# Conformer gates by the hyperbolic tangent, an earlier low part of the attention outputs, key copies from two queues

## The chip, the cores and the metric

The kernel runs on one core of one Trainium2 chip. The metric is the device time of one execution in microseconds; the kernel before took 2387.91 us in the median of 3 runs (2386.71 to 2388.96).

## The reference

One inference step of a two-layer streaming encoder, for 528 prompt frames (16 learned meta frames and 512) and 64 frames of a running stream, 592 columns in all. Per layer:

```python
xn = rmsnorm(x, p['norm1_g'])
proj = xn @ p['w_in']
q, k, v, sc_b, sc_c, sc_h, cf_a, cf_gate, gate_pre = jnp.split(proj, IN_SPLITS, axis=-1)
q = partial_rotary(q.reshape(n, l, N_Q_HEADS, HEAD_DIM), pos)
k = partial_rotary(k.reshape(n, l, N_KV_HEADS, HEAD_DIM), pos)
y_attn, new_k, new_v = attend(q, k, v, p['attn_sinks'])      # chunk-causal window, softmax with a sink per head
y_attn = y_attn @ p['w_attn_out']
...
glu = cf_a * jax.nn.sigmoid(cf_gate)
cf_conv, new_cf = causal_dwconv(glu, cf_hist, p['cf_conv_w'])    # 31 taps
y_cf = jax.nn.silu(layernorm(cf_conv, ...)) @ p['w_cf_out']
g_attn, g_sc, g_cf = jnp.split(jax.nn.sigmoid(gate_pre + p['b_gate']), 3, axis=-1)
x = x + (g_attn * y_attn + g_sc * y_sc + g_cf * y_cf) @ p['w_o']
...                                                              # a convolutional feed-forward block
```

D_MODEL is 1024, there are 16 query heads and 2 key/value heads of 64, and everything is float32.

## The kernel before, in words

Channels lie on the 128 partitions, frames along the free dimension. A weight matrix is cut into **panels** of 128 output channels by 1024 inputs, 174 per layer, which pass through in one fixed order. A panel is 8 **units** (one for each 128 inputs), and a unit is six matmuls: the float32 product is made of three passes, high weights by high input, high weights by low input, low weights by high input, each over two column pieces (L442). The high part of a panel's weights is written by ScalarE (`high`, L676), the low part by VectorE (`low`, L967); both have two buffers, so `high(w)` waits until TensorE has finished panel w-2, `low(w)` waits for `high(w)`, and TensorE waits for `low(w)` at the panel's first unit. SyncE issues the panels' loads.

Every engine's program is written out in order by hand, and each engine takes its instructions strictly in that order; waits are on semaphores. The change is in three places of a layer.

**The keys.** Panels 0 and 1 make keys and values, panels 2 to 9 the queries. The keys are rotated on VectorE (`k_rot`, L1046) and then copied twice into the buffer KD, one copy in each half of the partitions, by eight DMAs that SyncE issues one after another at panel 8 (L356, L357; for each of the 2 key heads and each half one large and one small). Before them on SyncE's queue stand the swaps for the first two queries and the load of panel 8, behind them the swaps for the next queries (L333, L334). ScalarE's `query(3)` (L733), which moves the result of a query panel out of PSUM into the place that the keys held, waits for all eight (`kd_in`), and TensorE's panel 7 waits for that PSUM tile. GpSimd copies the values (L400, L401) once VectorE has placed them (`vv_done`), and writes keys and values out after `kd_in`.

**The shade.** While TensorE runs panels 7 to 26 (160 units; the last queries and, as panels 10 to 25, eight pairs of a Conformer gate and a Conformer value), the attention is woven in. It has 20 items, one for each key head and chunk of frames; step s begins at unit 8 + 33 s // 5 (`STEP`), that is every six or seven units, and on TensorE it does `values(s - 3)`, `scores(s)`, `turn(s - 2)` (transposes). The other engines do their share at the same unit or one or two units (k) later:
- ScalarE at k = 1 `outputs_hi(s - 3)` and `copies(s - 2)`, at k = 2 `exps(s)` (one small and four large exponentials, L766 and L770);
- VectorE at k = 0 `divided(s - 1)` and `maxima(s)`, at k = 1 (and at k = 3 of odd steps, late in the shade) two convolution `taps` (L1157), and at k = 2 `outputs_lo(s - 3)` (L1119), the low part of an attention output.

TensorE's `scores(s)` waits for `exps(s - 1)`, since both use one PSUM region, and `values(i)` waits for `outputs_lo(i - 1)`. At each panel's start, ahead of the attention's share, ScalarE does `high` and then either a `query` or, at odd panels from 11 on, a Conformer gate: `gate` (L706), a Sigmoid from PSUM into scratch. VectorE does `low` and then a `rotation` of a query or, at even panels from 12 on, `glu` (L1141), the product of the gate and the value panel. Where a function that ScalarE needs is not in the table set that it holds, the compiled program has an ACT_TABLE_LOAD ahead of it; the profile gives it the line of the activation that needs it.

**Behind the shade**, panel 26 (N_OA) is the first of the branch gates, which are Sigmoids with a bias by the same `gate`.

Of the kernel before, what the change touches and what calls it, by code (L numbers as in the profile page):

```python
# [190 lines left out]
def encoder(nc, weights, xt, vecs, consts, kcache, vcache, cfhist, spill, y, kp, vp, scp, cfp, ffp, ks, vs):  # L191
# [18 lines left out]
    sums, rinv = sb("exp_sums", [128, 2, 4]), sb("inv_den", [128, 2, 4])  # L210
    warm = sb("warm", [128, 1])
    roots, inverse = sb("root_columns", [128, 2, 3]), sb("inverse_columns", [128, 2, 3])
# [68 lines left out]
    k_scaled, v_scaled, q_scaled, q1_tile = sem("k_scaled"), sem("v_scaled"), sem("q_scaled"), sem("q1_tile")  # L281
    k_cos, k_rot, kd_in = sem("k_cos"), sem("k_rot"), sem("kd_in")
    q_cos, q_sin, q_rot = sem("q_cos"), sem("q_sin"), sem("q_rot")
# [5 lines left out]
    o_done, oh_done, ol_done = sem("o_done"), sem("oh_done"), sem("ol_done")  # L289
    g_zero = sem("g_zero")  # L290
    tap_first, tap = sem("tap_first"), [sem(f"tap{g}") for g in range(4)]
# [16 lines left out]
    def tile_emptied(engine, key):  # L308
        s, before = USES[key]
        engine.wait_ge(out[s], before + 1)  # L310

    block = ctx.enter_context(nc.Block())
# [3 lines left out]
    def _(sp):  # L316
# [19 lines left out]
        for l in range(DEPTH):  # L336
            for n in range(PANELS):
# [13 lines left out]
                if n == 8:  # L351
                    sp.wait_ge(k_rot, l + 1)
                    for v in range(N_KV):
                        for h in (0, HEAD_DIM):
                            k = turning[HEAD_DIM * v:HEAD_DIM * v + HEAD_DIM, 0:TOK]
                            sp.dma_start(KD[h:h + HEAD_DIM, v, 0:TP], k[:, 0:TP]).then_inc(kd_in, 16)  # L356
                            sp.dma_start(KD[h:h + HEAD_DIM, v, TP + WINDOW:720], k[:, TP:TOK]).then_inc(kd_in, 16)  # L357
                if 8 <= n < 14:
# [15 lines left out]
    def _(pool):  # L374
        nc.gpsimd.memset(eps, EPS).then_inc(eps_set, 1)
        pool.dma_start(vs[:, 0:WINDOW - DEC_SEQ, :], vcache[:, DEC_SEQ:WINDOW, :]).then_inc(vs_out, 16)

# [8 lines left out]
        for l in range(DEPTH):  # L386
# [10 lines left out]
            pool.dma_start(VV[:, 7, 0, :], vcache[l, :, :]).then_inc(cache_in, 16)  # L397

            pool.wait_ge(vv_done, 2 * l + 2)
            pool.dma_start(VV[64:80, 0, 1, :], VV[0:16, 0, 1, :]).then_inc(v_twice, 16)  # L400
            pool.dma_start(VV[64:128, 1:8, 1, :], VV[0:64, 1:8, 1, :]).then_inc(v_twice, 16)  # L401
            pool.wait_ge(kd_in, (l + 1) * 128)
            pool.wait_ge(cache_in, (l + 1) * 32)
# [28 lines left out]
    def _(pe):  # L432
# [83 lines left out]
        def scores(l, i):  # L516
            v, c = divmod(i, CHUNKS)
            q0, k0, nk = chunk_span(c)
            g = l * ITEMS + i
            if i == 0:  # L520
                pe.wait_ge(q_rot, l * KT + 4)
                pe.wait_ge(vv_done, 2 * l + 2)
                pe.wait_ge(kd_in, (l + 1) * 128)
                pe.wait_ge(cache_in, (l + 1) * 32)
            if i == CHUNKS:
                pe.wait_ge(q_rot, l * KT + KT)
            if g:
                pe.wait_ge(p_done, g)
            for i2 in range(2):
                for e in range(2):  # L530
                    h = slice(64 * e, 64 * e + 64)
                    last = nc.tensor.matmul(scores_ps(nk)[:, e, i2, :], QI[h, 2 * v + i2, 2 * q0:2 * q0 + 128],  # L532
                                            KD[h, v, k0:k0 + nk], start=True, stop=True)
            last.then_inc(s_done, 1)
# [133 lines left out]
    def _(act):  # L668
# [33 lines left out]
        def gate(l, n, j, bias):  # L702
# [4 lines left out]
                .then_inc(out[USES[(l, n)][0]], 1)  # L707

        for m in range(KT):
            act.wait_ge(x_in[m], 16)  # L710
# [5 lines left out]
            square(m, m % 2, X[:, m, :], O_SQ, TOK)  # L716
        act.wait_ge(eps_set, 1)
        act.wait_ge(vec_in, 16)
        for l in range(DEPTH):
# [15 lines left out]
            def query(m):  # L735
                if m == 2:
                    act.wait_ge(vt_ps, 2 * l + 2)
                elif m == 3:
                    act.wait_ge(kd_in, (l + 1) * 128)
                elif m >= 4:  # L740
                    act.wait_ge(q_cos, l * KT + m - 3)
                    act.wait_ge(sw_in[place(m)], swaps(l, m - 4))
# [71 lines left out]
            for u in range(SHADE):  # L814
                n, k = N_SHADE + u // KT, u % KT
                if k == 0 and u:
# [3 lines left out]
                    elif (n - N_CF) % 2:  # L820
                        if n - N_CF >= 5:
                            tile_emptied(act, (l, n - 4))
                        gate(l, n - 1, (n - N_CF) // 2 % 2, 0.0)
                if n > N_CF and k == 5 and (n - N_CF) % 2 == 0:
# [132 lines left out]
    def _(dve):  # L957
# [46 lines left out]
        for l in range(DEPTH):  # L1004
# [118 lines left out]
            def attention_at(u):  # L1123
# [3 lines left out]
                if k == 0 and 0 <= s < ITEMS:  # L1127
                    maxima(s)
                if u > KT * (N_CF + 4 - N_SHADE) and (k == 1 or (k == 3 and s % 2)):
                    taps(1)  # L1130
                if k == 2 and 3 <= s:
                    outputs_lo(s - 3)

            def glu(m):
                tile_emptied(dve, (l, N_CF + 2 * m))
                dve.wait_ge(panel_done, W + N_CF + 2 * m + 2)
# [24 lines left out]
            for u in range(SHADE):  # L1161
                n, k = N_SHADE + u // KT, u % KT
                if k == 0 and u:
                    low(W + n + 1)
                    if n <= N_CF:
                        rotation(n - 2 - N_Q)
                    elif (n - N_CF) % 2 == 0:
                        glu((n - N_CF) // 2 - 1)
                if n == N_CF and k == 4:
                    rotation(KT - 1)  # L1170
                attention_at(u)

# [366 lines left out]
```

## Time and profile before

| | |
|---|---|
| median of 3 runs | 2387.91 us |
| the profiled execution | 2388.3 us, span 2387.0 us |
| TensorE matmuls busy | 2349.8 us (98%) |
| VectorE busy | 1598.5 us (67%) |
| ScalarE busy | 894.5 us (37%) |
| GpSimd busy | 43.6 us (2%) |
| mean granted TensorE clock | 0.998 of full speed |
| table loads | 52 of 1.283 us each, 38 of them at L706 and L766 |

The span runs from the first to the last instruction. An engine is busy while an instruction of its own executes; waiting for semaphores, and the issuing of DMAs, is not counted. Times in the trace are microseconds from the start of the span. The two layers are the same program; the second one's shade follows the first's by about 1191.7 us.

### The profile page before, as it was taken

The page shows a single profiled execution, that of the slowest core. Times are in us where ns is not written, and L with a number is a line of the kernel's source. Part 1 is how long each engine was busy: PE and PEld are TensorE (multiplying, and loading weights), DVE is VectorE, ACT ScalarE, POOL GpSimd, SP SyncE. Part 2 cuts the span into 40 slices and gives each one's busy share as a digit, 9 for nine tenths or more (in the row PEclk, how much of TensorE's full clock was granted, in tenths as well). Part 3 has the DMA queues.
Part 4 walks back from the last instruction along what each step waited for, and adds up shares of the span by engine and source line. Part 5 has one row for each costly group of instructions (what it writes and reads, how often), then busy time and mean ns, then how long its engine had stood idle before and what let it go on. Part 6 is the DMA issues. An engine that isn't in the chain of part 4 may idle for free.

```text
span 2387.0 us, 41935 instructions
## 1 busy us (share of the span) xinstructions
PE 2349.8 (98%) x17718; PEld 2313.9 (97%) x17718; DVE 1598.5 (67%) x2386; ACT 894.5 (37%) x1725; POOL 43.6 (2%) x74
## 2 busy tenths in 40 slices
PE   8999999999999999999999999999999999999998
PEld 8988999999999999999998889999999999999997
DVE  8677798885535664645776778999764356556366
ACT  5566222223523432423435662222244234334243
POOL 2000000000000000000010000000000000000000
PEclk9999999999999999999999999999999999999999
DMA  6211222222232222222242112222223322222222
GB/s 209 82 54 54 82 82 80 80 81 80 93 103 85 80 80 81 85 83 81 90 138 80 54 54 84 81 89 80 80 81 104 97 88 80 87 82 80 84 84 96
DMA packets 60028, 205.97 MB, mean 86 GB/s; under 512 B 8702, under 2 KB 10974, under 8 KB 59582
## 3 DMA queue, kind: packets, MB, share of 16 engines
q1 hardware_dynamic: 56448, 191.23, 24.8%
q0 software_dynamic: 3392, 12.05, 1.7%
q8 instruction: 140, 2.29, 0.4%
q14 instruction: 48, 0.39, 0.1%
HBM read 191.77 MB, written 8.50 MB: 84 GB/s over the span
## 4 chain that ended last, share of the span: by engine, by line
PE 91%; DVE 4%; ACT 2%; issue 1%; SPq 1%; DMA 1%; DVEq 0%; ACTq 0%
PE ps L442 87%; PE ps L532 1%; DVE w_lo L967 1%; PE ps L547 1%; PE ps L564 1%; ACT w_hi L676 1%; DVE xn_hi_lo L984 0%; DVE x_q_merged L1011 0%; PE ps L568 0%; ACT scratch L770 0%; DMA scratch<-cf_acc 0%; DVE scratch L979 0%; PE ps L470 0%; PE ps L550 0%; DVE cf_acc L1157 0%
## 5 line engine op out<-in xcount | busy, mean ns | idle before, releaser
L442 PE MATMUL ps<-xn_hi_lo,w_hi 128*128 128x288 f32 (+3 forms) x7552 | 1334.7, 299 | 12.9 <-DVE w_lo L967 9.6
L442 PEld LDWEIGHTS ps<-xn_hi_lo,w_hi 128*128 128x128 f32 x7552 | 1115.6, 188 | 15.8 <-issue 10.6
L442 PE MATMUL ps<-xn_hi_lo,w_lo 128*128 128x304 f32 (+2 forms) x3776 | 816.6, 298 | 0.0
L676 ACT ACTIVATE w_hi<-raw 128x1024 fp32r<-128x1024 f32 x348 | 369.3, 1061 | 1081.6 <-PE ps L442 1080.5
L967 DVE TENSOR_TENSOR w_lo<-raw,w_hi 128x1024 fp32r<-128x1024 f32 x348 | 426.0, 1224 | 519.6 <-ACT w_hi L676 519.4
L442 PEld LDWEIGHTS ps<-xn_hi_lo,w_lo 128*128 128x128 f32 x3776 | 605.7, 188 | 0.0
L442 PE MATMUL ps<-branch_hi_lo,w_hi 128*128 128x304 f32 (+2 forms) x2896 | 509.6, 298 | 4.3 <-DVE branch_hi_lo L1315 1.7
L442 PEld LDWEIGHTS ps<-branch_hi_lo,w_hi 128*128 128x128 f32 x2896 | 426.8, 188 | 7.1 <-issue 2.2
L1157 DVE SCALAR_TENSOR_TENSOR cf_acc<-glu,vec,cf_acc 128x622 f32<-128x622 f32 x480 | 383.6, 860 | 0.0
L442 PE MATMUL ps<-branch_hi_lo,w_lo 128*128 128x288 f32 (+2 forms) x1448 | 311.9, 297 | 0.0
L442 PEld LDWEIGHTS ps<-branch_hi_lo,w_lo 128*128 128x128 f32 x1448 | 232.2, 188 | 0.0
L1319 DVE SCALAR_TENSOR_TENSOR scratch<-scratch,vec 128x594 f32<-128x594 f32 x176 | 147.1, 836 | 18.6 <-ACT scratch L906 11.9
L1295 DVE TENSOR_TENSOR x_q_merged<-x_q_merged,ps 128x592 f32<-128x592 f32 (+2 forms) x62 | 47.3, 763 | 162.2 <-PE ps L442 162.0
L906 ACT ACTIVATE scratch<-scratch,vec 128x594 f32<-128x594 f32 x88 | 70.0, 796 | 153.4 <-DVE scratch L1325 153.4
L442 PE MATMUL ps<-merged_hi_lo,w_hi 128*128 128x288 f32 (+2 forms) x512 | 90.0, 298 | 0.3 <-DVE w_lo L967 0.2
L442 PEld LDWEIGHTS ps<-merged_hi_lo,w_hi 128*128 128x128 f32 x512 | 75.5, 188 | 0.7 <-issue 0.7
L1325 DVE TENSOR_TENSOR scratch<-scratch,ps 128x64 f32<-128x64 f32 (+2 forms) x176 | 72.2, 452 | 0.0
L770 ACT ACTIVATE scratch<-ps,neg_max 128x192 f32<-128x192 f32 (+3 forms) x160 | 60.0, 390 | 0.0
L442 PE MATMUL ps<-merged_hi_lo,w_lo 128*128 128x288 f32 (+2 forms) x256 | 55.3, 297 | 0.0
L975 DVE TENSOR_TENSOR scratch<-scratch 128x592 f32<-128x592 f32 (+1 forms) x54 | 42.1, 779 | 1.0
L984 DVE SCALAR_TENSOR_TENSOR xn_hi_lo<-x_q_merged,vec,xn_hi_lo 128x592 fp32r<-128x592 f32 x48 | 38.8, 827 | 4.6 <-ACT xn_hi_lo L713 4.6
L792 ACT ACTIVATE branch_hi_lo<-ps 128x128 fp32r<-128x128 f32 x80 | 17.8, 275 | 63.6 <-PE ps L550 50.3
(138 smaller groups left out, 1322.7 us busy)
## 6 DMA issues: line engine op xcount, KB each, us to landing
raw<-in_weights SPq DMA_DIRECT2D x348, 512.0 KB, 3.4
spill<-x_q_merged POOLq DMA_DIRECT2D x2, 2368.0 KB, 9.7
x_q_merged<-spill POOLq DMA_DIRECT2D x16, 296.0 KB, 3.1
x_q_merged<-in_xt SPq DMA_DIRECT2D x8, 296.0 KB, 7.0
cf_acc<-cf_acc SPq DMA_DIRECT2D x72, 18.5 KB
out_y<-x_q_merged SPq DMA_DIRECT2D x4, 304.0 KB, 2.4
out_y<-x_q_merged SPq DMA_DIRECT2D x4, 288.0 KB, 2.3
scratch<-cf_acc SPq DMA_DIRECT2D x8, 132.0 KB, 3.7
```

The costliest lines, as they stand in the source:

```text
L442: last = nc.tensor.matmul(to[:, t0:t1], a[:, w % 2, wk], both[:, part, k, t0:t1], start=(k == 0 and j == 0), stop=(k == nk - 1 and j == 2))
L532: last = nc.tensor.matmul(scores_ps(nk)[:, e, i2, :], QI[h, 2 * v + i2, 2 * q0:2 * q0 + 128], KD[h, v, k0:k0 + nk], start=True, stop=True)
L676: nc.scalar.activation(wh[:, w % 2, :], raw[:, w % 2, :], ACT.Copy).then_inc(hi_done, 1)
L770: last = nc.scalar.activation(scr[:, O_P + 768 * b + 192 * x:O_P + 768 * b + 192 * x + nk], scores_ps(nk)[:, x // 2, x % 2, :], ACT.Exp, b ...
L906: nc.scalar.activation(dst, src[:, 0:S_OUT], ACT.Identity, bias=0.0, scale=col(l, "ffw", m * 3)) \
L967: V.tensor_tensor(wl[:, w % 2, :], raw[:, w % 2, :], f(wh[:, w % 2, :]), ALU.subtract).then_inc(lo_done, 1)
L975: V.tensor_tensor(view(at, n), view(at, n), slot(sq, CF_OUT, s)[:, 0:n], ALU.add).then_inc(sq_sum, 1)
L984: V.scalar_tensor_tensor(xl[:, m, :], X[:, m, :], col(l, g, m), f(xh[:, m, :]), ALU.mult, ALU.subtract) \
L1157: V.scalar_tensor_tensor(acc[:, t, :], G[:, t, k + 1:k + 1 + CF_OUT], col(l, "cfw", t * CF_K + k + 1), acc[:, t, :], ALU.mult, ALU.add).th ...
L1295: V.tensor_tensor(X[:, m, t:], X[:, m, t:], ps((l, n0 + m))[:, t:], ALU.add) \
L1319: V.scalar_tensor_tensor(dst, src[:, k:k + S_OUT], col(l, "ffw", m * 3 + k), dst, ALU.mult, ALU.add) \
L1325: last = V.tensor_tensor(dst[:, o:o + w_], view(O_RF + t0_, w_), ps(key)[:, t0_:t0_ + w_], ALU.mult)
```

## The change

Three things, in both layers.

The Conformer gates become `sigmoid(x) = 0.5 tanh(x / 2) + 0.5`: a Tanh with scale 0.5 out of PSUM, a wait for its own end, and an Identity with scale 0.5 and a bias column of 0.5 in place. `glu` waits for the Identity by a semaphore of its own; the PSUM tile is still given free by the first of the two.

On VectorE, `outputs_lo(s - 3)` moves from k = 2 to k = 0, behind `maxima(s)` and ahead of the taps. At unit 8, the shade's first step, `maxima(0)` moves ahead of the rotation of a query.

Of the eight key copies, SyncE issues the four of key head 0 and GpSimd the four of key head 1, which there stand ahead of the copies of the values. The semaphore is split; the scores of key head 1 wait for theirs at item 10, ScalarE's `query(3)` and GpSimd's output of the keys wait for both.

```diff
-    k_cos, k_rot, kd_in = sem("k_cos"), sem("k_rot"), sem("kd_in")
+    k_cos, k_rot, kd_in = sem("k_cos"), sem("k_rot"), [sem("kd_in0"), sem("kd_in1")]
...
+    def keys_twice(engine, v):
+
+        k = turning[HEAD_DIM * v:HEAD_DIM * v + HEAD_DIM, 0:TOK]
+        for h in (0, HEAD_DIM):
+            engine.dma_start(KD[h:h + HEAD_DIM, v, 0:TP], k[:, 0:TP]).then_inc(kd_in[v], 16)
+            engine.dma_start(KD[h:h + HEAD_DIM, v, TP + WINDOW:720], k[:, TP:TOK]).then_inc(kd_in[v], 16)
...
                 if n == 8:
                     sp.wait_ge(k_rot, l + 1)
-                    for v in range(N_KV):
-                        for h in (0, HEAD_DIM):
-                            k = turning[HEAD_DIM * v:HEAD_DIM * v + HEAD_DIM, 0:TOK]
-                            sp.dma_start(KD[h:h + HEAD_DIM, v, 0:TP], k[:, 0:TP]).then_inc(kd_in, 16)
-                            sp.dma_start(KD[h:h + HEAD_DIM, v, TP + WINDOW:720], k[:, TP:TOK]).then_inc(kd_in, 16)
+                    keys_twice(sp, 0)
...
         nc.gpsimd.memset(eps, EPS).then_inc(eps_set, 1)
+        nc.gpsimd.memset(half[:, :], 0.5).then_inc(half_set, 1)
...
+            pool.wait_ge(k_rot, l + 1)
+            keys_twice(pool, 1)
             pool.wait_ge(vv_done, 2 * l + 2)
...
+        def tanh_gate(l, n, j):
+
+            act.wait_ge(panel_done, l * PANELS + n + 1)
+            to = slot(O_SG, TOK, j)
+            nc.scalar.activation(to, ps((l, n)), ACT.Tanh, scale=0.5).then_inc(out[USES[(l, n)][0]], 1)
+            tile_emptied(act, (l, n))
+            nc.scalar.activation(to, to, ACT.Identity, bias=half[:, :], scale=0.5).then_inc(sigmoid_done, 1)
...
-                        gate(l, n - 1, (n - N_CF) // 2 % 2, 0.0)
+                        tanh_gate(l, n - 1, (n - N_CF) // 2 % 2)
...
                     maxima(s)
+                if k == 0 and 3 <= s:
+                    outputs_lo(s - 3)
                 if u > KT * (N_CF + 4 - N_SHADE) and (k == 1 or (k == 3 and s % 2)):
                     taps(1)
-                if k == 2 and 3 <= s:
-                    outputs_lo(s - 3)
...
             def glu(m):
-                tile_emptied(dve, (l, N_CF + 2 * m))
+                dve.wait_ge(sigmoid_done, l * KT + m + 1)
...
                 if k == 0 and u:
                     low(W + n + 1)
+                if u == KT:
+                    attention_at(u)
+                if k == 0 and u:
                     if n <= N_CF:
                         rotation(n - 2 - N_Q)
...
-                attention_at(u)
+                if u != KT:
+                    attention_at(u)
```

## Rows read from the trace of the kernel before

**Rows 1.** The page, part 1: busy time, share, instructions.

```profile
PE 2349.8 (98%) x17718; PEld 2313.9 (97%) x17718; DVE 1598.5 (67%) x2386; ACT 894.5 (37%) x1725; POOL 43.6 (2%) x74
```

**Rows 2.** First layer's shade by stretch: length, PE, PEld, DVE, ACT, POOL busy, PEclk.

```profile
73.00:242.00 169.00, 163.46 (x1394) 149.38 (x1393) 120.38 (x274) 105.38 (x309) 0.00 (x0) 1.00 0.17 56
```

**Rows 3.** PE's waits, whole span: line, releaser, us in total, times, longest.

```profile
PE ps L532 <- ACT scratch L770: 6.9, 6, 1.4
PE ps L564 <- DVE branch_hi_lo L1119: 4.0, 6, 1.2
PE ps L442 <- ACT cf_acc L733: 3.2, 4, 1.4
```

**Rows 4.** PE's timeline: start, us, line, operation, [idle before, releaser].

```profile
61.25 0.80 PE L442 MATMUL ps<-xn_hi_lo,w_hi 128*128 128x304 f32 x4 [0.78 <-ACT cf_acc L733]
...
68.00 0.62 PE L532 MATMUL ps<-scratch,x_q_merged 64*128 64x16 f32 x8
...
74.58 0.68 PE L532 MATMUL ps<-scratch,x_q_merged 64*128 64x80 f32 x8 [0.86 <-ACT scratch L770]
...
121.49 0.92 PE L532 MATMUL ps<-scratch,x_q_merged 64*128 64x192 f32 x8 [1.40 <-ACT scratch L770]
...
168.99 0.65 PE L564 MATMUL ps<-scratch 16*64 16x128 f32 x8 [1.17 <-DVE branch_hi_lo L1119]
...
1252.92 0.81 PE L442 MATMUL ps<-xn_hi_lo,w_hi 128*128 128x304 f32 x4 [1.43 <-ACT cf_acc L733]
```

**Rows 5.** ACT's timeline ahead of PE's wait of 1.40 us.

```profile
115.25 1.28 ACT L706 ACT_TABLE_LOAD   x1
116.55 0.66 ACT L706 ACTIVATE scratch<-ps 128x592 f32<-128x592 f32 x1
...
118.33 1.28 ACT L766 ACT_TABLE_LOAD   x1
```

**Rows 6.** Groups by line, whole span: count, busy us, mean ns, idle before.

```profile
L706 ACT ACT_TABLE_LOAD x22 | 28.2, 1283 | 0.4
L766 ACT ACT_TABLE_LOAD x16 | 20.5, 1283 | 0.3
L693 ACT ACTIVATE xn_hi_lo<-x_q_merged,vec 128x592 fp32r<-128x592 f32 x24 | 18.6, 775 | 0.0
```

**Rows 7.** DVE's timeline ahead of PE's wait of 1.17 us.

```profile
164.91 1.23 DVE L967 TENSOR_TENSOR w_lo<-raw,w_hi 128x1024 fp32r<-128x1024 f32 x1 [1.35 <-ACT w_hi L676]
...
168.36 0.48 DVE L1119 TENSOR_TENSOR branch_hi_lo<-ps,branch_hi_lo 128x128 fp32r<-128x128 f32 x2
```

**Rows 8.** ACT's timeline at the same place: the second of the two `copies`.

```profile
165.40 0.25 ACT L783 ACTIVATE scratch<-ps 16x128 f32<-16x128 f32 x1
```

**Rows 9.** DVE's timeline ahead of PE's wait of 0.86 us.

```profile
69.26 1.23 DVE L967 TENSOR_TENSOR w_lo<-raw,w_hi 128x1024 fp32r<-128x1024 f32 x1 [1.81 <-ACT w_hi L676]
...
72.66 0.22 DVE L1081 TENSOR_REDUCE score_max<-ps 128x4 f32<-128x64 f32 x1
```

**Rows 10.** SP's timeline: the fourth of the eight key copies.

```profile
54.22 0.60 SPq L357 DMA_DIRECT2D scratch<-cf_acc  x1
```

**Rows 11.** The chain that ended last: from the eighth key copy to query(3).

```profile
56.80 3.70 DMA scratch<-cf_acc
...
60.53 0.67 ACT cf_acc L733
```

**Rows 12.** POOL's timeline: its copies of the values.

```profile
54.62 0.53 POOL L400 DMA_DIRECT2D scratch<-scratch  x1 [22.09 <-DVE scratch L1065]
55.14 0.78 POOL L401 DMA_DIRECT2D scratch<-scratch  x1
```

**Rows 13.** DMA issues by line: queue, count, KB each, median us to landing.

```profile
scratch<-scratch POOLq DMA_DIRECT2D x2, 224.0 KB, 4.5
```

**Rows 14.** DVE's timeline: the end of the keys' rotation, and of query 3's.

```profile
51.23 0.78 DVE L1046 TENSOR_TENSOR cf_acc<-cf_acc 128x592 f32<-128x592 f32 x1
...
65.80 0.77 DVE L1056 TENSOR_TENSOR cf_acc<-cf_acc,cos_sin 128x592 f32<-128x592 f32 x1 [0.66 <-DMA cf_acc<-cf_acc]
```

More of the change, by code:

```diff
@@ L210, in encoder @@
     sums, rinv = sb("exp_sums", [128, 2, 4]), sb("inv_den", [128, 2, 4])
-    warm = sb("warm", [128, 1])
+    warm, half = sb("warm", [128, 1]), sb("half", [128, 1])
     roots, inverse = sb("root_columns", [128, 2, 3]), sb("inverse_columns", [128, 2, 3])
@@ L289, in encoder @@
     o_done, oh_done, ol_done = sem("o_done"), sem("oh_done"), sem("ol_done")
-    g_zero = sem("g_zero")
+    g_zero, half_set, sigmoid_done = sem("g_zero"), sem("half_set"), sem("sigmoid_done")
     tap_first, tap = sem("tap_first"), [sem(f"tap{g}") for g in range(4)]
@@ L401, in _ @@
             pool.dma_start(VV[64:128, 1:8, 1, :], VV[0:64, 1:8, 1, :]).then_inc(v_twice, 16)
-            pool.wait_ge(kd_in, (l + 1) * 128)
+            pool.wait_ge(kd_in[0], (l + 1) * 64)
+            pool.wait_ge(kd_in[1], (l + 1) * 64)
             pool.wait_ge(cache_in, (l + 1) * 32)
@@ L522, in scores @@
                 pe.wait_ge(vv_done, 2 * l + 2)
-                pe.wait_ge(kd_in, (l + 1) * 128)
+                pe.wait_ge(kd_in[0], (l + 1) * 64)
                 pe.wait_ge(cache_in, (l + 1) * 32)
             if i == CHUNKS:
+                pe.wait_ge(kd_in[1], (l + 1) * 64)
                 pe.wait_ge(q_rot, l * KT + KT)
@@ L717, in _ @@
         act.wait_ge(eps_set, 1)
+        act.wait_ge(half_set, 1)
         act.wait_ge(vec_in, 16)
@@ L738, in query @@
                 elif m == 3:
-                    act.wait_ge(kd_in, (l + 1) * 128)
+                    act.wait_ge(kd_in[0], (l + 1) * 64)
+                    act.wait_ge(kd_in[1], (l + 1) * 64)
                 elif m >= 4:
```

## The prediction

> **What bounds the kernel now.** I began with the busy shares: TensorE's matmuls fill 98% of the span, and no other engine comes near it [rows 1]. So an edit can only pay where TensorE stands idle, and the second view is the list of its waits [rows 3]. Three of its lines lie in the parts that the change touches: the scores waiting for the exponentials (6.9 us over six times), the values waiting for the outputs' low part (4.0 over six), and panels waiting for a PSUM tile that ScalarE moves out (3.2 over four). The third view, by stretches, confirms the size: in the first layer's shade TensorE is idle for 169.00 - 163.46 = 5.54 us [rows 2], and half of 6.9 + 4.0 is 5.45. The fourth view, TensorE's timeline, tells where each wait stands [rows 4]; the second layer repeats the first's six within 0.01 us. Scores: 0.86 at step 1, 1.40 at step 7, and the rest of the half, 3.45 - 2.26 = 1.19, at step 19. Low part: 1.17 at step 13, and the rest of 2.0, 0.83, over steps 8 and 18. Tile: of the four waits on L733 the two at panel 7 are 0.78 and 1.43; the other two, 1.0 together, lie earlier and are not touched. Last, for each of these waits, I read the waiting chain's timeline.
>
> **Tanh instead of Sigmoid.** In the shade each of the eight gates of a layer loads its table (1.28 us), and the next exponentials load theirs back: 16 loads of the 22 at L706, all 16 at L766 [rows 6]. If Tanh is in the exponential's set, one exponential load per layer stays, and one Sigmoid load moves to the first branch gate, panel 26. That is 28 loads less, 28 x 1.283 = 35.9 us of ScalarE, against 16 Identities with a bias column, priced at 775 ns by the row of the same shape [rows 6], 12.4 us: ScalarE's busy time should fall from 894.5 [rows 1] to about 871. For the span only the chain ahead of a wait counts. At step 7 it runs w_hi, load, Sigmoid, outputs and copies, load, exponentials [rows 5]. Each load costs 1.30 from start to next start (115.25 to 116.55). The Identity adds 0.78, and its wait for the Tanh's end something that no row of this kind shows: I bound it by 0 and 0.10, the nearest being the 0.03 between the last landing (56.80 + 3.70) and ScalarE's start at 60.53 [rows 11], and take 0.06. So the exponentials end 2.60 - 0.84 = 1.76 us earlier, more than the 1.40 at step 7 and the 1.19 at step 19. Both waits go, with 0.36 and 0.57 to spare: 2 x 2.59 = **5.2 us**.
> What is late next? `glu` now waits for the Identity, which ends 1.30 - 0.84 earlier than the Sigmoid did, so nothing there. The load at panel 26 stands ahead of work that is asked for a panel later, and a panel takes 6.75 us (61.25 to 68.00 [rows 4]); uncovered it would cost 1.3 per layer.
>
> **The outputs' low part ahead of the taps.** At step 13 TensorE asked at 168.99 - 1.17 = 167.82, and the low part ran from 168.36 to 168.84, since w_lo, glu and a pair of taps stood ahead of it [rows 7]. In the new order it stands behind `maxima(12)`, where it waits for ScalarE's copies, which end at 165.65 [rows 8]: it is done at about 166.2, 1.6 us before it is asked for. The waits at steps 8 and 18 are of the same kind with 0.4 each. Gain 2 x 2.0 = **4.0 us**.
> The price: while VectorE waits for the copies, everything behind waits too. Here it is w_lo, from 164.91 to about 166.15, then glu and the taps by about 0.8. The next panel needs this w_lo only at its own start; VectorE has 169.0 - 120.4 = 48.6 us of idle time in the shade [rows 2], 2.4 per step, to catch up. I cost it at nothing; where w_lo is overtaken (steps 6, 7, 12 and 18) the bound is the third rival.
>
> **First maxima ahead of the rotation.** w_lo ends at 70.49, and the maxima start at 72.66 only because a rotation lies between [rows 9]. They move 2.17 forward, the wait is 0.86 [rows 4], and all of it goes: 2 x 0.86 = **1.7 us**. The rotation is delayed by the 0.6 of the maxima; its query is used at item 10, far away.
>
> **Keys' copies.** SyncE issues eight, the last at 56.80, landing 3.70 later, and `query(3)` starts at 60.53 [rows 11]. Now SyncE's last is the fourth, at 54.22 [rows 10]: landing at 57.9 by the same 3.70. GpSimd's four can begin when the keys are rotated, 51.23 + 0.78 = 52.0 [rows 14]; at 0.53 to 0.78 an issue [rows 12] the last starts at 53.6 to 54.4, and lands 3.7 [rows 11] to 4.5 later, the latter for the larger copy from this queue [rows 13]: 57.3 to 58.9. I take 58.4, about 2.1 us sooner. TensorE needs 0.78 in the first layer and 1.43 in the second [rows 4], so both waits go: **2.2 us**.
> Queues passed: GpSimd's copies of the values, at 54.62 before [rows 12], come at 54.1 to 55.1, and nothing asks for them before step 3, 19 units behind 68.00. SyncE's swaps for queries 2 and 3 and its next panels come up to 2.6 earlier. That matters, because the scores of item 0, at 68.00 [rows 4], now come at 67.22 and need query 3 rotated: before, that rotation waited 0.66 for its swap [rows 14] and ended at about 67.4. The swap stands behind `query(3)`, which comes 2.1 earlier, so that wait should go and the rotation end at 66.8. If it stayed, 0.2 us would come back per layer.
>
> **The sum.** 5.2 + 4.0 + 1.7 + 2.2 = 13.1 us. The profiled execution took 2388.3, its span 2387.0 and 1.3 around it, which the change doesn't touch: 2375.2. The median of the runs lies 0.4 below that execution, so 2374.8, and I say **2375**. A change under 0.2%, 4.8 us, can't be told from none.
>
> **Rivals.**
> *GpSimd's queue doesn't help* (0.13). Its issues might be held up by what VectorE does at the time, placing the values out of PSUM. For: of two neighbouring issues one took 0.53 and the next 0.78 [rows 12]. Against: 0.25 is all that shows. If the four only begin when the values are placed (54.62) and take 0.78 each, the last starts at 56.9 and lands at 60.6 to 61.4, against 60.50 now: the waits come to 0.9 to 1.7 and 1.5 to 2.3, and the time to 2377.5 to 2379.2 (0.4 less for the median). The Trainium skill has such a rule, "SBUF — State Buffer", section "SBUF: two separate sides": a transfer issued from GpSimd can't get its descriptors written while VectorE holds the port that they share in a two-port copy. No row shows whether these copies hold it; by that rule it would be this rival.
> *The tables stay* (0.05): the change doesn't do what it says, because Tanh is taken from another set than the exponential's. No row has a Tanh, so the trace doesn't decide it. Then both loads stay in each chain and the Identity comes on top: waits of 1.40 + 0.84 and 1.19 + 0.84 per layer, 8.5 in all, 2383.7. The Trainium skill ("ScalarE: Activation LUTs", section "Table sets: the hidden batching unit") lists tanh in the exponential's set and in the sigmoid's; no run here shows it yet.
> *VectorE is blocked* (0.02, slower). At steps 6, 7, 12 and 18 w_lo now stands behind a low part that waits for ScalarE's w_hi, gate, outputs and copies. At step 6 these end at 118.33 [rows 5] - 1.30 + 0.84 = 117.9, w_lo ends at 117.9 + 0.5 + 1.2 = 119.6, and its panel begins two units and the attention's share behind 121.49 - 1.40 = 120.09, at 122.6 at the soonest: 3.0 spare. It makes the kernel slower from 13.1 / 8 = 1.6 beyond that, if the low part held VectorE 4.6 us longer at all eight places; at 6 longer it gives 2375.2 + 8 x 3.0 = 2399. Nothing in the rows is that long.
> *Small waits come back* (0.09): the three thinnest spares (0.36 at step 7, 0.4 at the first scores, 0.57 at step 19) are overdrawn by 0.3 to 0.6 in both layers, 2376.5 to 2378.5.
>
> **How the numbers follow.** The forecast has 0.71, between 2373 (the runs' spread below, and the 0.09 per shade that the listed waits leave over) and 2376.5. The small waits and GpSimd's queue reach to 2379; with them 0.9 is covered, and the range is 2373 to 2379. The tables' case lies at the bound of "same". Faster 0.94, same 0.04, slower 0.02.
>
> **What would show it.** Right: no load at L706's Conformer gates and 24 in place of 52 in the kernel, ScalarE busy near 871; TensorE's waits on L770 and L1119 gone from the list, and no new ones in their place; TensorE idle in each shade under 0.5 us; `query(3)` starting near 58.4; the stretches outside unchanged. Wrong: a wait of TensorE on w_lo at a panel's start inside the shade (VectorE blocked), scores still waiting for the exponentials at steps 7 and 19 (chain longer than priced), or `query(3)` still at 60.5.

## The result, and the profile after

The changed kernel takes 2374.55 us in the median of 6 runs (2374.43 to 2375.10); the kernel before, beside it, 2388.05 (2386.71 to 2389.02). The ratio is 0.9943, with an interval of 0.9932 to 0.9954: faster by 13.5 us, where 12.9 had been forecast. The profiled execution took 2375.1, its span is 2373.8.

Read it as before: the busy shares, then TensorE's waits, then the shade. The page's first part, of after:

```profile
PE 2348.4 (99%) x17718; PEld 2314.1 (97%) x17718; DVE 1598.5 (67%) x2386; ACT 869.6 (37%) x1713; POOL 47.6 (2%) x83
```

ScalarE lost 24.9 us [rows 1]; TensorE's busy time fell by 1.4 with the same instructions, which matters further down. TensorE's waits of after (line, releaser, us in total, times, longest):

```profile
PE ps L449 <- DVE w_lo L985: 11.3, 7, 10.1
...
PE ps L449 <- ACT cf_acc L750: 1.0, 2, 0.6
```

All three lines of [rows 3] are answered here: the scores' wait for the exponentials and the values' wait for the low part are gone, and of the panels' wait for a PSUM tile only the two earlier ones are left, 1.0 together. No line inside the shades is new (the 10.1 is the wait for the first weights, at the start). The first layer's shade by stretch, from panel 7 on (length, then PE, PEld, DVE, ACT, POOL busy, granted clock):

```profile
61.20:236.30 175.10, 175.10 (x1487) 161.33 (x1485) 130.70 (x288) 96.03 (x307) 3.64 (x7) 1.00 0.20 64
```

TensorE is busy for all of it, where 5.54 us of idle time stood before from 73 us on [rows 2] and 0.78 at panel 7 [rows 4].

**Where the time went.** Two stretches of each execution hold all that the change touches: from ScalarE's first load for the square root to the start of the long unbroken TensorE run behind the first shade, and from the run of 234 at the end of the first layer to the same point of the second. The chain that ended last gives them; before, then after:

```profile
23.14 1.28 ACT L697
...
241.77 293.40 PE ps L442 x2154
...
1172.47 32.07 PE ps L442 x234
...
1433.40 287.14 PE ps L442 x2154
```

```profile
24.98 1.28 ACT L705
...
236.46 293.40 PE ps L449 x2154
...
1167.34 32.11 PE ps L449 x234
...
1420.56 287.14 PE ps L449 x2154
```

Before: 218.63 + 260.93 = 479.56 us. After: 211.48 + 253.22 = 464.70. So 14.9 us went, where the listed idle time of the fourteen waits is 13.1. The rest of the span took back 1.7: the start is 1.84 us later in this execution, the remaining pieces -0.2 in sum.

### The profile page after: what moved, and what is told of

Read it like the earlier page. It is cut to its first block, busy times and chain, and to the rows that moved or that the text cites. A ratio compares the mean times of both kernels' runs of the same rounds, so it can differ in the third digit from the quotient of the medians.

```text
span 2373.8 us, 41924 instructions
## 1 busy us (share of the span) xinstructions
PE 2348.4 (99%) x17718; PEld 2314.1 (97%) x17718; DVE 1598.5 (67%) x2386; ACT 869.6 (37%) x1713; POOL 47.6 (2%) x83
## 3 DMA queue, kind: packets, MB, share of 16 engines
q1 hardware_dynamic: 55808, 190.63, 24.9%
## 4 chain that ended last, share of the span: by engine, by line
PE 97%; DVE 1%; ACT 1%; DMA 0%; issue 0%; SPq 0%; DVEq 0%; ACTq 0%
PE ps L449 92%; PE ps L540 1%; PE ps L572 1%; PE ps L555 1%; ACT w_hi L684 1%; DVE w_lo L985 1%; PE ps L576 1%; PE ps L477 0%; PE ps L558 0%; PE ps L463 0%; DMA raw<-in_weights 0%; DVE x_q_merged L1401 0%; DVE scratch L1341 0%; PE ps L615 0%; ACT L705 0%
## 5 line engine op out<-in xcount | busy, mean ns | idle before, releaser
L449 PE MATMUL ps<-xn_hi_lo,w_hi 128*128 128x288 f32 (+3 forms) x7552 | 1334.9, 299 | 11.7 <-DVE w_lo L985 10.5
L449 PEld LDWEIGHTS ps<-merged_hi_lo,w_lo 128*128 128x128 f32 x256 | 41.3, 189 | 0.0
```

What stands on the lines that cost most here:

```text
L449: last = nc.tensor.matmul(to[:, t0:t1], a[:, w % 2, wk], both[:, part, k, t0:t1], start=(k == 0 and j == 0), stop=(k == nk - 1 and j == 2))
```

## The experiments

Each kernel is compared with the one before (2387.9 to 2388.2 in the medians beside them) or with the changed one. "Stretches" are the two above, in the profiled execution; "idle" is the sum of the waits listed there.

**One part alone.** Three kernels carry one part each on top of the kernel before, a fourth the low part's move without the maxima's.

*Tanh alone.* The call at L823 becomes `tanh_gate`, and `glu` waits for `sigmoid_done`:

```
-                        gate(l, n - 1, (n - N_CF) // 2 % 2, 0.0)
+                        tanh_gate(l, n - 1, (n - N_CF) // 2 % 2)
...
-                tile_emptied(dve, (l, N_CF + 2 * m))
+                dve.wait_ge(sigmoid_done, l * KT + m + 1)
```

> The kernel before with the Tanh gates alone. Theory A (the forecast's: a wait of TensorE is worth the idle time that the profile lists, and the parts add up): the waits of the scores at steps 7 and 19 go, 2 x 2.59 = 5.2 us, those at steps 1, 8, 13, 18 and at panel 7 stay as they were; 2388.05 - 5.2 = 2382.9. Theory B (a wait costs about 0.13 us more than its listed idle time, because TensorE is slow for a moment after it; in the changed kernel the two stretches from the end of panel 6 to the end of the shade became 14.93 us shorter, where 13.10 of idle time was listed over 14 waits): 5.2 + 4 x 0.13 = 5.7, 2382.3. Theory C (the parts overlap: with one wait gone another grows): less than 4 us, and the waits on the low part listed at more than 4.0 us. Table loads: 24 instead of 52, ScalarE busy 870.

Measured: 2382.8 us, ratio 0.9978 (0.9969 to 0.9987), 5.4 less. TensorE's waits:

```profile
PE ps L565 <- DVE branch_hi_lo L1129: 4.0, 6, 1.2
...
PE ps L533 <- ACT scratch L780: 1.7, 2, 0.9
```

The four waits of steps 7 and 19 are gone: of the scores' 6.9 the two at step 1 are left. The tile's line reads 2.8 in place of 3.2; its two waits at panel 7 differ from execution to execution, as will show below.

*The order alone.* The low part straight behind the maxima, and the first maxima ahead of the rotation:

```
+                if k == 0 and 3 <= s:
+                    outputs_lo(s - 3)
...
-                if k == 2 and 3 <= s:
-                    outputs_lo(s - 3)
...
+                if u == KT:
+                    attention_at(u)
...
-                attention_at(u)
+                if u != KT:
+                    attention_at(u)
```

> The kernel before with VectorE's new order alone (the low part behind the maxima, the first maxima ahead of the rotation). Theory A: the waits at steps 1, 8, 13 and 18 go, 4.0 + 1.7 = 5.7 us, 2382.3; those at steps 7 and 19 stay at 1.40 and 1.20. Theory B: 5.7 + 8 x 0.13 = 6.7, 2381.3. Theory C: the waits at steps 7 and 19 grow, less than 5 us. If VectorE is blocked by the low part's wait for ScalarE (which is longer here than with Tanh, because the loads stand in ScalarE's way), waits of TensorE on w_lo at a panel's start appear inside the shade.

Measured: 2381.56 us, ratio 0.9972 (0.9961 to 0.9983), 6.6 less.

```profile
PE ps L532 <- ACT scratch L770: 5.0, 4, 1.4
...
PE ps L564 <- DVE branch_hi_lo L1119: 0.2, 1, 0.2
```

The low part's waits fall from 4.0 to 0.2. What is left is in the first layer, at values 4: one of the two loads still lies ahead of ScalarE's copies, and a low part that no longer waits for taps waits for these copies instead. Nothing is lost by it here, since the scores of step 7 behind it wait 0.2 less (1.19, before 1.40).

*The low part's move alone* is the first two blocks of that diff.

> The kernel before with the outputs' low part behind the maxima and ahead of the taps as the only edit; the first maxima stay behind the rotation. Theory A (listed idle): the waits on the low part go, 4.0 us, but for one of 0.2 at values 4 in the first layer as with both moves: 2384.4. Theory B (0.13 us more for each wait gone): 5 waits net, 2383.8. Rival (the low part ahead of the convolution's taps delays the gates' products, and the gain goes): 2388. Against the run with both moves, 2381.6, the first maxima are then worth 2.2 to 2.8, where their idle time is 1.7.

Measured: 2383.23 us, ratio 0.9978 (0.9969 to 0.9988), 4.8 less; the maxima's move is the other 1.7 by the medians. In the profiled execution, the shortest of the ten (2382.03), the stretches are 5.5 shorter, but only 3.8 of that is the low part's line. The two waits at panel 7 are 0.8 shorter there, one of 0.7 for query 3's rotation comes in, and the wait at step 1 of the second layer behind it shrinks from 0.85 to 0.13.

*The keys' copies alone*: `keys_twice(sp, 0)` on SyncE, `keys_twice(pool, 1)` on GpSimd ahead of its copies of the values, a semaphore for each key head.

> The kernel before with the keys' copies from two queues alone. Theory A: the two waits at panel 7, 0.78 and 1.43, go: 2.2 us, 2385.8. Theory B: 2.2 + 0.26 = 2.5, 2385.6. Theory C: the gain is given back at the first scores, which come sooner and wait for a query's rotation or for the exponentials: 1 us or less. The copies' landing: 3.7 us from issue if the two queues don't hinder each other, about 4.9, as in the changed kernel's trace, if they share the DMA engines' time.

Measured: 2386.49 us, ratio 0.9992 (0.9983 to 1.0001), 1.7 less: on its own this part isn't told from no change. The tile's line falls to the two early waits, 1.0, and nothing else moves.

The parts add up: 5.4 + 6.6 + 1.7 = 13.7, against 13.5 for all; by stretches 6.0 + 6.8 + 2.5 = 15.3, against 14.9. Theory C, an overlap between the parts, doesn't show: the stretches leave 0.4 for it. The medians alone couldn't tell, with intervals of some 2 us to either side.

**One part undone.** *The changed kernel with the eight copies on SyncE again:*

```
-                    keys_twice(sp, 0)
+                    for v in range(N_KV):
+                        for h in (0, HEAD_DIM):
+                            k = turning[HEAD_DIM * v:HEAD_DIM * v + HEAD_DIM, 0:TOK]
+                            sp.dma_start(KD[h:h + HEAD_DIM, v, 0:TP], k[:, 0:TP]).then_inc(kd_in, 16)
...
-            pool.wait_ge(k_rot, l + 1)
-            keys_twice(pool, 1)
```

> The changed kernel with all eight key copies from SyncE again. Theory A: 2374.55 + 2.2 = 2376.8, with the two waits of 0.78 and 1.43 at panel 7 back and no others. Theory B: 2377.0. Theory C (the keys' part is hidden once the others are in): 2374.6 to 2375.5.

Measured: 2375.91 us, ratio 0.9948 (0.9934 to 0.9962): 1.4 above the changed kernel in the medians, less than theory A (2376.8) and B (2377.0) have, and 3.4 by the stretches of the profiled execution, the longest of the five. TensorE's timeline (start, us, instruction, idle before):

```profile
62.10 0.81 PE L443 MATMUL ps<-xn_hi_lo,w_hi 128*128 128x304 f32 x4 [1.20 <-ACT cf_acc L743]
...
1247.33 0.81 PE L443 MATMUL ps<-xn_hi_lo,w_hi 128*128 128x304 f32 x4 [0.82 <-ACT cf_acc L743]
...
1254.90 0.62 PE L533 MATMUL ps<-scratch,x_q_merged 64*128 64x16 f32 x8 [0.74 <-DVE x_q_merged L1069]
```

These waits differ from execution to execution (0.78 and 1.43 before, [rows 4]). Here, and in the run with the low part alone, the second one is short (0.82 and 0.84), and the first scores wait for query 3's rotation a panel later: the late `query(3)` is then paid at both places.

*The changed kernel with the first maxima behind the rotation:*

```
-                if u == KT:
-                    attention_at(u)
...
-                if u != KT:
-                    attention_at(u)
+                attention_at(u)
```

> The changed kernel with the first maxima of each half behind the rotation again, as in the kernel before; all else as changed. Theory A: the wait of 0.86 at step 1 comes back in both layers and nothing else, 1.7 us, 2376.3. Theory B (0.13 us more for each wait): 2.0 us, 2376.5. Rival (the maxima's place is hidden by what follows): no wait, 2374.6. By the stretch from the end of panel 6 to the shade's end, 174.14 us in the changed kernel's both layers, it can be told more finely: 175.00 by A, 175.13 by B.

Measured: 2376.31 us, ratio 0.9950 (0.9937 to 0.9962), 1.8 above the changed kernel (2.3 by the stretches). The wait is back at its old size in both layers, with no other in the list; one of 0.10 at the first layer's panel 7 is too short for it:

```profile
74.65 0.68 PE L540 MATMUL ps<-scratch,x_q_merged 64*128 64x80 f32 x8 [0.86 <-ACT scratch L788]
```

**The rivals, made on purpose.** *The tables stay:*

```
-            nc.scalar.activation(to, ps((l, n)), ACT.Tanh, scale=0.5).then_inc(out[USES[(l, n)][0]], 1)
+            nc.scalar.activation(to, ps((l, n)), ACT.Sigmoid).then_inc(out[USES[(l, n)][0]], 1)
...
-            nc.scalar.activation(to, to, ACT.Identity, bias=half[:, :], scale=0.5).then_inc(sigmoid_done, 1)
+            nc.scalar.activation(to, to, ACT.Identity, bias=half[:, :], scale=1.0).then_inc(sigmoid_done, 1)
```

with `half` set to 0.

> The changed kernel with the gates' Sigmoid kept: the Identity behind it multiplies by 1 and adds 0, so the same numbers come out. This is the case of the prediction's second rival, made on purpose: both table loads stay in ScalarE's chain (16 at the gates, 16 at the exponentials) and the Identity lies on top. Theory A (a wait costs the idle time listed for it): the chain grows by 2 x 1.30 against the changed kernel's, whose spares are about 0.5 at step 7 and 0.8 at step 19, so waits of 2.1 and 1.8 a layer come at the scores, and one of 0.7 on the low part behind them in the first layer: 8.5 us in all, about 2383.0. Theory B (each wait costs 0.13 us more than is listed): four or five waits more, 2383.6. Rival: the order of the low part and the keys' copies absorb the longer chain, and the time stays under 2380. ScalarE's busy time should be near 907 us (894.5 + 16 x 0.78), with 52 loads.

Measured: 2386.26 us (2385.04 to 2389.48), ratio 0.9993 (0.9984 to 1.0002); ScalarE busy 907.4 us. The waits came out as worked out in their sum, 8.5 us:

```profile
PE ps L540 <- ACT scratch L788: 6.6, 4, 2.0
PE ps L572 <- DVE branch_hi_lo L1137: 1.9, 2, 1.0
```

Their places are others than expected. In both layers the low part waits at values 4 (1.05 and 0.83) and the scores of step 7 behind it for the rest (1.19 and 1.41): 2.24 a layer, as the prediction had it for step 7 alone.

But the kernel is 11.7 above the changed one, not 8.5. In the profiled execution, one of the shorter (2385.13), the stretches are 10.45 longer, and the granted clock tells most of the difference. TensorE's timeline at step 19 of the first layer, and stretches of 2 us from there on:

```profile
217.12 0.92 PE L540 MATMUL ps<-scratch,x_q_merged 64*128 64x192 f32 x8 [2.01 <-ACT scratch L788]
```

```profile
216.00:218.00 2.00, 0.88 (x9) 0.65 (x9) 0.83 (x3) 1.07 (x6) 0.00 (x0) 0.98 0.08 31
218.00:220.00 2.00, 2.00 (x11) 2.00 (x10) 1.80 (x6) 0.39 (x3) 0.00 (x0) 0.50 0.00 0
220.00:222.00 2.00, 2.00 (x12) 2.00 (x11) 1.07 (x3) 2.00 (x11) 0.00 (x0) 0.67 0.02 4
```

Behind the idle 2.01 us the clock was at 0.50, the 1.2 GHz level, and came back by 222: 2 x 0.02 + 2 x 0.50 + 2 x 0.33 = 1.7 us lost. 8.5 + 1.7 = 10.2 of 10.45; the rest is of the size of what a wait costs beside its idle time (see the sum, below). The second layer has the same wait of 2.01 and a clock of 1.00 behind it. Whether this is chance a second execution of the same kernel was to tell:

> A second profiled execution of the kernel with Sigmoid kept. The first listed 8.5 us of waits and showed TensorE's clock at 0.50 for some 3.4 us behind the wait of 2.0 at step 19 of the first layer, worth 1.7 us, and at 1.00 behind the same wait of the second layer. Theory (such a fall comes by chance behind a wait of about 2 us): the same waits to 0.05, and falls at none, one or both of the two step 19 waits, the time moving by 1.7 for each. Rival (the fall belongs to this place of the program): again in the first layer and not in the second.

Measured: 2385.49 us, the same 6.6 and 1.9 of waits, and the fall again in the first layer (0.55 and 0.60 in the two stretches from 218 on) and not in the second. So the rival of that run held: in two of two executions the fall belongs to the place. What in the place decides it, no run here shows, and what the executions of up to 2389.48 us had on top of these two, no trace shows either.

*GpSimd's key copies behind its copies of the values:*

```
-            pool.wait_ge(k_rot, l + 1)
-            keys_twice(pool, 1)
             pool.wait_ge(vv_done, 2 * l + 2)
...
+            pool.wait_ge(k_rot, l + 1)
+            keys_twice(pool, 1)
```

> The changed kernel with GpSimd's four key copies behind its copies of the values, that is behind the point at which VectorE has placed the values (about 54.6 us in the kernel before). It is the place from which the prediction's first rival priced a queue that doesn't help. That rival's working: the last of the four starts at 56.3 to 56.9 on the clock of the kernel before, lands 3.7 to 4.5 later, waits of 0.9 to 1.7 and 1.5 to 2.3 at panel 7, 2377.5 to 2379.2 less 0.4. Theory from the changed kernel's trace, where an issue takes 0.55 and a landing 4.7 to 5.3 because two queues share the way: two issues more stand ahead, the last key lands 1.1 later than in the changed kernel, where it came 1.5 us sooner than in the kernel before: 0.4 sooner than before, waits of 0.4 and 0.8 to 1.0 a layer, 2375.8 to 2376.2.

Measured: 2378.47 us, ratio 0.9960 (0.9947 to 0.9972), 3.9 above the changed kernel. The timelines of GpSimd (first and last of its key copies) and of TensorE:

```profile
57.34 0.57 POOL L316 DMA_DIRECT2D scratch<-cf_acc  x1
...
58.89 0.55 POOL L317 DMA_DIRECT2D scratch<-cf_acc  x1
```

```profile
64.19 0.81 PE L449 MATMUL ps<-xn_hi_lo,w_hi 128*128 128x304 f32 x4 [2.27 <-ACT cf_acc L750]
...
1250.31 0.86 PE L449 MATMUL ps<-xn_hi_lo,w_hi 128*128 128x304 f32 x4 [1.75 <-ACT cf_acc L750]
```

The waits are 4.0 us, the upper end of what the prediction's first rival priced (1.7 + 2.3), and the time lies in its range; the expectation from the changed kernel's trace, 2376, missed. It counted the two issues ahead (0.53 + 0.78 us) but not that GpSimd begins only at 56.06, when the values are placed; the keys are rotated 2.6 us before (52.68 + 0.78). In this kernel the granted clock falls behind the wait of 1.75 in the second layer (0.50 in the stretch from 1252 to 1254) and stays at 1.00 behind the longer one of 2.27 in the first. The profiled execution is the longest of the five (2380.81, the others 2378.36 to 2378.55), so the median needn't hold this fall.

**The spares.** *The changed kernel with one more Copy in ScalarE's chain:*

```
             nc.scalar.activation(to, to, ACT.Identity, bias=half[:, :], scale=0.5).then_inc(sigmoid_done, 1)
+            act.wait_ge(sigmoid_done, l * KT + (n - N_CF) // 2 + 1)
+            nc.scalar.activation(to, to, ACT.Copy).then_inc(second_done, 1)
...
-                dve.wait_ge(sigmoid_done, l * KT + m + 1)
+                dve.wait_ge(second_done, l * KT + m + 1)
```

> The changed kernel with one more instruction of ScalarE in the chain: a Copy of the gate onto itself behind the Identity, for which the gate's product waits. It measures the spares of steps 7 and 19. The copy should take what the Identity takes, 0.69 to 0.80 from start to next start. Theory A (spares as read in the changed kernel's trace, 0.5 and 0.8): a wait of 0.2 to 0.3 at step 7 and none or 0.1 at step 19, in both layers: 0.4 to 0.8 us, 2375.0 to 2375.4. Rival (spares as the prediction worked them out, 0.36 and 0.57): waits of 0.4 and 0.2 a layer, 1.2 us, 2375.8. If no wait shows, both spares are over 0.8. ScalarE's busy time grows by 16 x 0.79 = 12.6 us to 882.

Measured: 2374.75 us, ratio 0.9942 (0.9929 to 0.9954), 0.2 above the changed kernel. The chain is 0.74 longer at each gate, and one wait shows in the list in the shades, in the first layer:

```profile
117.50 0.66 PE L572 MATMUL ps<-scratch 128*64 128x128 f32 x8 [0.35 <-DVE branch_hi_lo L1139]
```

It is not on the exponentials but, as in the run with the order alone, on the low part, which waits for ScalarE's copies; behind it the scores come late enough to find their exponentials done. At step 19 these end at 212.59, 0.09 ahead of the scores.

**The start.** *The changed kernel once more:*

> A second profiled execution of the changed kernel. In the first one the start, up to ScalarE's first table load for the square root, ended at 24.98 us, 1.85 later than in the kernel before. Theory (the landing of the first weights differs from execution to execution, and the change has no part in it): anywhere from 23.1 to 25.0, the span by as much shorter than 2373.8, and no wait of TensorE in the shades. Rival (the change makes the start longer): again 24.9 to 25.1, 2373.8.

Measured: 2374.69 us, span 2373.4, no wait in the shades, and both stretches again 211.48 and 253.22. ScalarE's first load here:

```profile
24.04 1.28 ACT L705 ACT_TABLE_LOAD   x1
```

One program has 24.98 and 24.04, so half of the 1.84 us belongs to the execution. Of the 1.84, 1.2 is the landing of the first weights (4.78 us before, 6.00 after) and 0.6 the first 78 matmuls, which took 13.0 us before and 13.6 after; in the second execution of the changed kernel the landing took 5.67 and the matmuls 13.0 again. All the profiled executions of kernels that hold all of the change, or all but one part, lie between 23.38 and 24.98, those of the other kernels between 23.14 and 24.68. Whether the change has a small share in it stays open.

## Why the prediction was right

**Tanh (forecast 5.2; alone 5.4, by stretches 6.0).** The mechanism is the one forecast. The table loads of after at the gates and in the shade (count, busy us, mean ns, idle before), and the Identity:

```profile
L714 ACT ACT_TABLE_LOAD x8 | 10.3, 1283 | 0.1
...
L784 ACT ACT_TABLE_LOAD x2 | 2.6, 1283 | 0.0
...
L723 ACT ACTIVATE scratch<-scratch,half 128x592 f32<-128x592 f32 x16 | 12.6, 790 | 0.5
```

With the unchanged ones that makes 24 loads in all, and ScalarE's 869.6 meets the 871. The trace agrees with the Trainium skill here ("ScalarE: Activation LUTs", "Table sets: the hidden batching unit"): Tanh and the exponential share a set, since no load stands between them. Of the terms the chain was mis-sized. ScalarE's timeline of after at step 6, and TensorE's scores behind it:

```profile
113.89 1.06 ACT L684 ACTIVATE w_hi<-raw 128x1024 fp32r<-128x1024 f32 x1 [3.44 <-PE ps L449]
114.86 0.65 ACT L721 ACTIVATE scratch<-ps 128x592 f32<-128x592 f32 x1
115.54 0.79 ACT L723 ACTIVATE scratch<-scratch,half 128x592 f32<-128x592 f32 x1
116.23 0.43 ACT L810 ACTIVATE branch_hi_lo<-ps 128x128 fp32r<-128x128 f32 x2
...
117.28 0.23 ACT L784 ACTIVATE sink_exp<-sink_diff 128x4 f32<-128x4 f32 x1
...
118.87 0.25 ACT L788 ACTIVATION_READ_ACCUMULATOR scratch<-ps,neg_max 128x1 f32 x1
```

```profile
119.65 0.92 PE L540 MATMUL ps<-scratch,x_q_merged 64*128 64x192 f32 x8
```

ScalarE's timeline of before at the same place; the loads and the Sigmoid between these are in [rows 5]:

```profile
114.17 1.06 ACT L676 ACTIVATE w_hi<-raw 128x1024 fp32r<-128x1024 f32 x1 [3.43 <-PE ps L442]
...
117.11 0.44 ACT L792 ACTIVATE branch_hi_lo<-ps 128x128 fp32r<-128x128 f32 x2
...
119.63 0.21 ACT L766 ACTIVATE sink_exp<-sink_diff 128x4 f32<-128x4 f32 x1
...
121.23 0.21 ACT L770 ACTIVATION_READ_ACCUMULATOR scratch<-ps,neg_max 128x1 f32 x1
```

From w_hi's start to the exponentials' end it is 5.23, before 7.27: 2.04 saved where 1.76 was forecast. From start to start, w_hi to the gate takes 0.97 where it took 2.38, the gate itself 1.37 where it took 0.56, and outputs and copies up to the first exponential 1.05 where they took 2.52. So the Identity with its wait cost 0.81, close to the 0.84 of the prediction. What was mis-sized is the loads: priced at 1.30 each, they were worth 1.41 and 1.47. Without a load the next instruction starts before the one ahead has ended (0.97 after w_hi's start, and w_hi takes 1.06); a load started behind that end (115.25 against 114.17 + 1.06). The spare at step 7 is 119.65 - 119.12 = 0.53 (forecast 0.36) and at step 19, by the same rows, 0.83 (0.57). The run with one Copy more bears it out: its 0.74 left 0.09 at step 19, and at step 7 would overdraw the spare by 0.2, which the 0.35 us ahead of it covers. In the changed kernel itself none of the three thin spares of the prediction's fourth rival is overdrawn (the third is the 0.43 of the first scores, below).

**Low part (4.0; alone 4.8, by its line of waits 3.8).** VectorE's timeline at step 12, and TensorE's values at step 13:

```profile
163.42 0.49 DVE L1137 TENSOR_TENSOR branch_hi_lo<-ps,branch_hi_lo 128x128 fp32r<-128x128 f32 x2 [2.19 <-ACT scratch L801]
163.83 1.22 DVE L985 TENSOR_TENSOR w_lo<-raw,w_hi 128x1024 fp32r<-128x1024 f32 x1
```

```profile
165.41 0.65 PE L572 MATMUL ps<-scratch 16*64 16x128 f32 x8
```

The low part is done at 163.91, 1.5 us ahead of the values (forecast 1.6), with w_lo right behind it and the taps later, as in the working from [rows 7]. VectorE stood 2.19 us for the copies and nobody missed it: no wait on w_lo in the shades, so the third rival has nothing for it. At step 6 w_lo ended at 119.36, over 3 us ahead of its panel, as worked out.

**First maxima (1.7; undone 1.8).** They start at 71.20, where w_lo ends, instead of behind a rotation [rows 9]:

```profile
70.05 1.22 DVE L985 TENSOR_TENSOR w_lo<-raw,w_hi 128x1024 fp32r<-128x1024 f32 x1 [1.71 <-ACT w_hi L684]
71.20 0.22 DVE L1099 TENSOR_REDUCE score_max<-ps 128x4 f32<-128x64 f32 x1
```

**Keys' copies (2.2; alone 1.7, undone 1.4).** The waits went, with less to spare than was worked out. GpSimd's timeline (first and last of its key copies) and VectorE's beside it:

```profile
54.16 0.55 POOL L316 DMA_DIRECT2D scratch<-cf_acc  x1 [19.79 <-DVE cf_acc L1064]
...
55.73 0.55 POOL L317 DMA_DIRECT2D scratch<-cf_acc  x1
```

```profile
53.78 2.40 DVE L1083 COPY scratch<-ps 128x512 f32<-128x512 f32 x5
```

Four issues at 0.55 us or less while VectorE copies the values out of PSUM: the issues were not held, and the first rival's reason falls as far as they go (its price, for copies that do come late, held). The hold that the Trainium skill describes ("SBUF — State Buffer", "SBUF: two separate sides") doesn't show here; its example is a copy from SBUF to SBUF, these read PSUM, so the rule is neither borne out nor refuted. What was mis-sized is the landing. DMA issues between 50 and 64 us (KB each, median us to landing), of after and then of the kernel with GpSimd's copies late:

```profile
scratch<-cf_acc SPq DMA_DIRECT2D x2, 132.0 KB, 4.9
scratch<-cf_acc POOLq DMA_DIRECT2D x2, 132.0 KB, 4.4
```

```profile
scratch<-cf_acc SPq DMA_DIRECT2D x2, 132.0 KB, 3.5
scratch<-cf_acc POOLq DMA_DIRECT2D x2, 132.0 KB, 3.0
```

The prediction carried the 3.70 of one queue [rows 11] over to two that run at once. Side by side SyncE's take 4.9; with GpSimd's out of the way, 3.5: it is the company and not the queue. GpSimd's landings are longer by the same 1.4, so nothing marks them as held, though a hold of some tenths behind the issues isn't excluded. The last to land were SyncE's (issued at 55.94, 4.9 later), where the prediction had GpSimd's. `query(3)` started at 60.86, on before's clock 59.01: 1.5 sooner, not 2.1. That still covers what TensorE needed, and the first scores came 0.43 behind query 3's rotation, as forecast (0.4).

**The sum.** 13.1 was forecast and 13.5 measured, but the terms are larger: the stretches give more than the idle time listed, 6.0 for 5.7 (Tanh), 6.8 for 6.0 (order), 2.5 for 2.2 (keys), 14.9 for 13.1 (all), about 0.13 us per wait over the fourteen. That mean hides two sizes. TensorE's group ahead of the scores of step 7, before and then after:

```profile
119.64 0.45 PE L568 MATMUL ps<-scratch 64*64 64x128 f32 x8
```

```profile
119.27 0.45 PE L576 MATMUL ps<-scratch 64*64 64x128 f32 x8
```

After, the scores start at 119.65, 0.38 behind this group's start and 0.07 before its end. Before, they start at 121.49 [rows 4], 1.85 behind it, of which 1.40 is listed. The idle time is counted from the end of the last matmul, so the overlap of 0.07 that a wait takes away isn't in it. With the traces laid side by side, instruction by instruction, the same 0.07 stands at every wait of the attention, from 0.02 to 2.01 us long, and 0.26 at a wait at panel 7: 0.16 of lost overlap and 0.10 in the slower matmuls behind it. Sixteen of the one and two of the other, with the idle time of the four among them that are too short for the list (0.2 together), make 1.8, the whole difference. So theory B had the mean right, but its reason, a TensorE that is slow after a wait, holds only for the 0.10 at panel 7. TensorE's busy time, which fell by 1.4 us for the same instructions, points the same way. Against this larger gain stood the later start. The forecast was good partly by luck: an underrated gain and a start-up that it didn't consider had opposite signs.

**The tables' price** was the weakest number of the prediction: 2383.7 for a case that the chip ran at 2386.3. The sum of the idle time was right (8.5), its price wasn't: it left out the fall of the clock behind one of the two waits of 2.01, 1.7 us in the traced executions (2385.1 and 2385.5), and the 0.07 of each wait. For the rest of the median there is no trace.

## What to carry over

When one engine is busy 98% of the time, list its waits, find for each the chain that releases it and the slack on that chain after the edit: the parts then add up (13.7 for 13.5). Price the overlap that a wait or a table load takes away as well as its own length. A part that moves work forward needs the next releaser checked too: the low part, once ahead of the taps, waits for ScalarE's copies. A landing time read from one queue was too short here once two ran at once (3.7 carried over, 4.9 measured).

## What the hardware showed beyond the forecast

- Two queues copying at the same time: 4.9 and 4.4 us to landing for 132 KB, against 3.6 for one queue before and 3.5 and 3.0 one after the other.
- The granted clock fell to 0.50 for about 3 us behind waits of 2.01 (first layer, in both executions) and 1.75 us, and not behind another of 2.01 and one of 2.27. Each fall cost about 1.7 us by the granted clock.
- A wait of TensorE cost more than its listed idle time: 0.07 us in the attention, whatever its length, and 0.26 at panel 7.
- A table load of 1.28 us lengthened ScalarE's chain by 1.41 and 1.47 us, since its neighbours no longer overlap.
- The first weights landed after 4.78 to 6.00 us, which moved everything behind them.
